# Splitting the 512-column matmuls of a two-block transformer kernel into pairs of 256, with their input laid out anew

## The reference

```python
# layer A and layer B, 512 tokens
qkv = x @ w_qkv                       # 1024 -> 3072
mix = attention(q, k, v) @ w_o        # 1024 -> 1024
x = layer_norm(DEEPNORM_ALPHA * x + mix, ...)
gate, up = jnp.split(x @ w_in, 2, axis=-1)      # 1024 -> 2 * 2816
x = layer_norm(DEEPNORM_ALPHA * x + (silu(gate) * up) @ w_out, ...)
# the second model: 16 meta tokens + 512 tokens = 528 columns
```

## Time and profile before

| | |
|---|---|
| median of 3 runs | 2583.98 us (2582.28 to 2586.15) |
| the profiled execution's own time | 2582.26 us |
| its span, first to last instruction | 2580.5 us |
| TensorE busy | 2535.2 us, 98% |
| VectorE busy | 1622.0 us, 63% |
| ScalarE busy | 1163.0 us, 45% |
| mean granted TensorE clock | 0.997 |

### The profile page before, as it was taken

The page is one execution under the profiler, slowest core; times in us unless marked ns, Lnnn a source line. Parts: engine busy times, 40 slices in busy tenths (PEclk is TensorE's granted clock), DMA queues, the critical chain, the costliest instruction groups (busy, mean ns, idle before and its releaser), DMA issues.

```text
span 2580.5 us, 44843 instructions
## 1 busy us (share of the span) xinstructions
PE 2535.2 (98%) x19310; PEld 2300.2 (89%) x19310; DVE 1622.0 (63%) x2784; ACT 1163.0 (45%) x1924; POOL 168.7 (7%) x218
## 2 busy tenths in 40 slices
PE   9999999999999999999999999999999999999998
PEld 7777889889877888989899899999999989999998
DVE  6767746457566665546766456666675754766666
ACT  4554533335455443334554444434454534544443
POOL 0000200100000110110000001001000000200100
PEclk9999999999999999999999999999999999999999
DMA  5221955974322492795311149359652112954965
GB/s 193 89 63 70 260 143 161 293 185 147 108 73 74 151 253 84 261 257 161 141 67 65 60 142 263 98 170 289 158 189 92 65 64 103 260 144 136 293 174 162
DMA packets 104280, 397.39 MB, mean 154 GB/s; under 512 B 10401, under 2 KB 12705, under 8 KB 84241
## 3 DMA queue, kind: packets, MB, share of 16 engines
q1 hardware_dynamic: 60400, 249.07, 28.1%
q0 software_dynamic: 42960, 143.88, 23.7%
q10 hardware_dynamic: 720, 1.57, 0.2%
HBM read 383.87 MB, written 133.30 MB: 200 GB/s over the span
## 4 chain that ended last, share of the span: by engine, by line
PE 89%; DVE 6%; ACT 3%; DMA 1%; issue 1%; SPq 0%; DVEq 0%; ACTq 0%
PE P L684 60%; PE P L1014 13%; PE P L802 4%; PE P L780 3%; PE P L691 2%; DVE WL L2115 2%; ACT WH L1473 1%; PE P L814 1%; DMA raw<-in_wts 1%; PE P L1111 1%; PE P L1132 1%; PE P L1224 1%; PE P L828 1%; PE P L860 1%; DVE X L2210 0%
## 5 line engine op out<-in xcount | busy, mean ns | idle before, releaser
L684 PE MATMUL P<-XH,WL 128*128 128x264 f32 (+3 forms) x3080 | 843.0, 323 | 15.3 <-DVE XL L2448 6.9
L684 PE MATMUL P<-XL,WH 128*128 128x264 f32 (+3 forms) x3080 | 823.1, 316 | 0.0
L684 PE MATMUL P<-XH,WH 128*128 128x264 f32 (+3 forms) x3080 | 820.4, 315 | 0.0
L2115 DVE TENSOR_TENSOR WL<-raw,WH 128x1024 fp32r<-128x1024 f32 (+2 forms) x533 | 573.7, 1079 | 326.5 <-ACT WH L1473 325.0
L1473 ACT ACTIVATE WH<-raw 128x1024 fp32r<-128x1024 f32 (+2 forms) x533 | 497.9, 940 | 467.7 <-PE P L684 228.7
L684 PEld LDWEIGHTS P<-XH,WL 128*128 128x128 f32 x3080 | 520.4, 188 | 65.6 <-DVE XL L2448 9.8
L684 PEld LDWEIGHTS P<-XH,WH 128*128 128x128 f32 x3080 | 518.9, 189 | 37.8
L684 PEld LDWEIGHTS P<-XL,WH 128*128 128x128 f32 x3080 | 519.0, 188 | 36.6
L1014 PE MATMUL P<-GHH,WL 128*128 128x264 f32 (+1 forms) x616 | 176.2, 286 | 9.7 <-DVE WL L2115 9.7
L1014 PE MATMUL P<-GHL,WH 128*128 128x264 f32 (+1 forms) x616 | 175.4, 285 | 0.0
L1014 PE MATMUL P<-GHH,WH 128*128 128x264 f32 (+1 forms) x616 | 175.3, 285 | 0.0
(11 more groups left out here) (372 smaller groups left out, 3803.6 us busy)
## 6 DMA issues: line engine op xcount, KB each, us to landing
raw<-in_wts SPq DMA_DIRECT2D x151, 1024.0 KB, 5.1
sums<-in_quads POOLq DMA_DIRECT2D x32, 1152.0 KB, 28.4
sums<-in_quads POOLq DMA_DIRECT2D x32, 960.0 KB, 24.1
sums<-in_quads POOLq DMA_DIRECT2D x16, 1536.0 KB, 19.1
raw<-sums SPq DMA_DIRECT2D x64, 384.0 KB, 3.4
sums<-in_quads POOLq DMA_DIRECT2D x16, 1280.0 KB, 12.9
raw<-sums SPq DMA_DIRECT2D x64, 320.0 KB, 3.1
raw<-in_wts SPq DMA_DIRECT2D x48, 384.0 KB, 3.6
```

The lines of the kernel that those rows point to most:

```text
L684: ins = nc.tensor.matmul(P[:, a:a + x1 - x0], wb[:, s, 128 * k:128 * k + 128], xb[:, kx, x0 - c0:x1 - c0], start=start and i == 0, stop=st ...
L2115: nc.vector.tensor_tensor(WL[:, u % NS, 0:length(u)], raw_of(u), WH[:, u % NS, 0:length(u)].bitcast(F), ALU.subtract).then_inc(*dve.up("wl ...
```

## The change

Three things. `one(b)` gives two segments of 256 columns in place of one of 512, in the same bank. The input gets views `XHf` and `XLf` on the memory of `XH` and `XL`, with rows of 512 columns (2048 bytes) for the eight steps; `XHf` starts where `XH` does, `XLf` 128 columns (512 bytes) into `XL`, so that the low part is 17408 bytes (17 KiB) behind the high one. All writers and readers of the input in the 512-token stages take these views; the stages on 528 tokens keep `XH` and `XL`. Only the first matmul of a bank clears it.

```diff
 def one(b):
-    return [(512 * b, META, T)]
+    return [in_bank(b, a0, a1) for a0, a1 in HV]
...
+        XHf, XLf = (x[:, :, :].rearrange("p k t -> p (k t)")[:, a:a + 4096].rearrange("p (k t) -> p k t", t=512)
+                    for x, a in ((XH, 0), (XL, 128)))
...
                 for i, (wb, xb) in enumerate(((WL, xh), (WH, xl), (WH, xh))):
                     for a, x0, x1 in segs:
+                        first_of_bank = all(a // 512 != b // 512 for b, x2, _ in segs if x2 < x0)
                         ins = nc.tensor.matmul(P[:, a:a + x1 - x0], wb[:, s, 128 * k:128 * k + 128],
-                                               xb[:, kx, x0 - c0:x1 - c0], start=start and i == 0, stop=stop and i == 2,
-                                               skip_group_check=loose)
+                                               xb[:, kx, x0 - c0:x1 - c0], start=start and i == 0 and first_of_bank, stop=stop and i == 2,
+                                               skip_group_check=loose or len({b // 512 for b, _, _ in segs}) < len(segs))
...
+                xh, xl, c0 = (XHf, XLf, META) if one_bank else (XH, XL, 0)
...
-                        part(u, k, [seg(0, 0)], XH, XL, k, 0, k == 0, k == 7, True)
+                        part(u, k, [seg(0, 0)], xh, xl, k, c0, k == 0, k == 7, True)
...
-                            for i, (xb, wb) in enumerate(((XL, WH), (XH, WL), (XH, WH))):
-                                ins = nc.tensor.matmul(o, xb[:, k, c0:c1], wb[:, (u + k // 4) % NS, 256 * (k % 4):256 * (k % 4) + 256],
+                            for i, (xb, wb) in enumerate(((XLf, WH), (XHf, WL), (XHf, WH))):
+                                ins = nc.tensor.matmul(o, xb[:, k, c0 - META:c1 - META], wb[:, (u + k // 4) % NS, 256 * (k % 4):256 * (k % 4) + 256],
...
-                        tile(U + 6 * g + n, one(b), XH, XL, slot)
+                        tile(U + 6 * g + n, one(b), XHf, XLf, slot, META)
...
-                        tile(up_unit(U, n), one(b), XH, XL)
+                        tile(up_unit(U, n), one(b), XHf, XLf, c0=META)
...
-                nc.scalar.activation(XH[:, m, a:b], tmp[m % 4][:, a:b], ACT.Identity, bias=par("ln_b", 16 * (s // 2) + 8 * (s % 2) + m)
+                nc.scalar.activation(XHf[:, m, a - META:b - META], tmp[m % 4][:, a:b], ACT.Identity, bias=par("ln_b", 16 * (s // 2) + 8 * (s % 2) + m)
```

More of the change, by code:

```diff
@@ L705, in early @@
                         pe.wait_ge(*at("xl", 0, k))
-                        ins = part(u + n, k, regions[n], XH, XL, k, 0, k == 0, k == 7)
+                        ins = part(u + n, k, regions[n], XHf, XLf, k, META, k == 0, k == 7)
                     ins.then_inc(*pe.up("unit", u + n))
             def early_halves(u, seg, ver, one_bank, between, late=()):
+                xh, xl, c0 = (XHf, XLf, META) if one_bank else (XH, XL, 0)
                 pe.wait_ge(*at("wlo", u))
@@ L715, in early_halves @@
                         pe.wait_ge(*at("xl", ver, k, 0))
-                        part(u, k, [seg(0, 0)], XH, XL, k, 0, k == 0, k == 7, True)
+                        part(u, k, [seg(0, 0)], xh, xl, k, c0, k == 0, k == 7, True)
                     if k >= 2:
                         pe.wait_ge(*at("wlo", u + 1))
-                        part(u + 1, k - 2, [seg(1, 0)], XH, XL, k - 2, 0, k == 2, k == 9, True)
+                        part(u + 1, k - 2, [seg(1, 0)], xh, xl, k - 2, c0, k == 2, k == 9, True)
                     if k < 8:
@@ L723, in early_halves @@
                 for k in range(8):
-                    part(u + 2, k, [seg(2, 0)], XH, XL, k, 0, k == 0, k == 7, True)
+                    part(u + 2, k, [seg(2, 0)], xh, xl, k, c0, k == 0, k == 7, True)
                     between(1, k)
@@ L730, in early_halves @@
                         for n in ns:
-                            ins = part(u + n, k, [seg(n, 1)], XH, XL, k, 0, k == 0 and not one_bank, k == 7, True)
+                            ins = part(u + n, k, [seg(n, 1)], xh, xl, k, c0, k == 0 and not one_bank, k == 7, True)
                             if k == 7:
@@ L2081, in act_program @@
                 act.wait_ge(x_loaded[k], 16)
-                nc.scalar.activation(XH[:, k, C1], X[:, k, C1], ACT.Copy).then_inc(*act.up("xh", 0, k))
+                nc.scalar.activation(XHf[:, k, :], X[:, k, C1], ACT.Copy).then_inc(*act.up("xh", 0, k))
                 if k == 2:
@@ L2226, in split @@
                 dve.wait_ge(*at("xh", s + 1, m, hf))
-                nc.vector.scalar_tensor_tensor(XL[:, m, a:b], tmp[m % 4][:, a:b], par("ln_b", 16 * (s // 2) + 8 * (s % 2) + m),
-                                               XH[:, m, a:b].bitcast(F), ALU.add, ALU.subtract).then_inc(*dve.up("xl", s + 1, m, hf))
+                nc.vector.scalar_tensor_tensor(XLf[:, m, a - META:b - META], tmp[m % 4][:, a:b], par("ln_b", 16 * (s // 2) + 8 * (s % 2) + m),
+                                               XHf[:, m, a - META:b - META].bitcast(F), ALU.add, ALU.subtract).then_inc(*dve.up("xl", s + 1, m, hf))
             def layer_norm(s, U):
@@ L2243, in layer_norm @@
                     else:
-                        nc.vector.scalar_tensor_tensor(X[:, m, C1], XH[:, m, C1].bitcast(F), float(ALPHA), pb, ALU.mult, ALU.add
+                        nc.vector.scalar_tensor_tensor(X[:, m, C1], XHf[:, m, :].bitcast(F), float(ALPHA), pb, ALU.mult, ALU.add
                                                        ).then_inc(*dve.up("reshi", s, m))
                         dve.wait_ge(*at("reshi", s, m))
-                        nc.vector.scalar_tensor_tensor(X[:, m, C1], XL[:, m, C1].bitcast(F), float(ALPHA), X[:, m, C1],
+                        nc.vector.scalar_tensor_tensor(X[:, m, C1], XLf[:, m, :].bitcast(F), float(ALPHA), X[:, m, C1],
                                                        ALU.mult, ALU.add).then_inc(*dve.up("res", s, m))
@@ L2468, in feed_forward @@
                         k = n // 2 - 2
-                        nc.vector.tensor_tensor(X[:, k, C1], XH[:, k, C1].bitcast(F), XL[:, k, C1].bitcast(F), ALU.add
+                        nc.vector.tensor_tensor(X[:, k, C1], XHf[:, k, :].bitcast(F), XLf[:, k, :].bitcast(F), ALU.add
                                                 ).then_inc(*dve.up("xs", l, k))
@@ L2603, in partial @@
                 dve.wait_ge(*at("apv", 2, 1))
-                nc.vector.scalar_tensor_tensor(parts[n], XH[:, n, C1].bitcast(F).rearrange(halves, c=256), float(ALPHA),
+                nc.vector.scalar_tensor_tensor(parts[n], XHf[:, n, :].bitcast(F).rearrange(halves, c=256), float(ALPHA),
                                                bank(n).rearrange(halves, c=256), ALU.mult, ALU.add).then_inc(*dve.up("part", s, n))
                 dve.wait_ge(*at("part", s, n))
-                nc.vector.scalar_tensor_tensor(parts[n], XL[:, n, C1].bitcast(F).rearrange(halves, c=256), float(ALPHA), parts[n],
+                nc.vector.scalar_tensor_tensor(parts[n], XLf[:, n, :].bitcast(F).rearrange(halves, c=256), float(ALPHA), parts[n],
                                                ALU.mult, ALU.add).then_inc(*dve.up("partlo", s, n))
@@ L2994, in dve_program @@
                 dve.wait_ge(*at("xh", 0, k))
-                nc.vector.tensor_tensor(XL[:, k, C1], X[:, k, C1], XH[:, k, C1].bitcast(F), ALU.subtract).then_inc(*dve.up("xl", 0, k))
+                nc.vector.tensor_tensor(XLf[:, k, :], X[:, k, C1], XHf[:, k, :].bitcast(F), ALU.subtract).then_inc(*dve.up("xl", 0, k))
                 if k == 2:
```

4 lines of the change are left out of this document (2 added, 2 removed).

## The result

The changed kernel takes 2607.57 us in the median (2606.93 to 2610.72), the kernel before 2584.24 (2582.28 to 2586.15), four executions each: a ratio of 1.009, with a 95% interval of 1.0078 to 1.0101. It is slower by 23.3 us; forecast were +17.5 us and 2601 us. The profiled execution took 2606.93 us, its span is 2605.1 us, 24.6 more than before, at the same mean granted clock of 0.997.

The account below looks back on a forecast made before the run. TensorE was taken as the bound, busy 2535.2 of 2580.5 us; 16.8 + 0.8 + 0.6 - 0.7 = +17.5 us gave 2601 us. Its own range was 2592 to 2609 us; for eight times in ten, from 2566 to 2609.

Parts of the forecast that it names:

- points 5, 6 and 7: More matmuls and loads to issue, the other engines' work, and waits: each priced at nothing.
- Point 1: Dense tiles on `XH`: 2664 matmuls of 512 columns become 5328 of 256 at 119 ns, +16.8 us.
- at 120: Matmuls at equal phases take 120 ns: dense tiles +22.1 us, `values_of` +1.6, `early_halves` +1.0.
- Points 2 and 3: `values_of` (768 matmuls) and `early_halves` (432), all at 119 ns: +0.8 us and +0.6 us.
- Point 4: Output projections: 288 matmuls of 512 columns become pairs, half at the fast and half at the slow speed, -0.7 us.
- The fast speed: Rival: uniform rows run at 113.3 ns throughout, -20.7 us, 2563 us; chance 0.27 for throughout or nearly.
- The mixture: Rival: speed depends on the last disturbance, stages fall on either side, about -2 us, 2582 us; chance 0.11.
- One price per matmul: Rival: each extra matmul costs a fixed 3.7 ns, +10.9 us, 2595 us; chance 0.17 together with the plain slow speed.

Follow-up runs that it names:

- pad64: The changed kernel with 64 unused bytes ahead of the weights, which move to phase 192 while the input stays at 128; 2580.23 us, ratio 0.9986 to the kernel before.
- shift64: The changed kernel with the input views started 48 columns into `XH` and 112 into `XL`, so streamed rows have phase 64; 2582.14 us, ratio 0.9982 to the kernel before.
- spacing: The changed kernel with `XLf` at the start of `XL`, so the low part is 16.5 KiB behind the high one, phases equal as before; 2607.85 us.
- layout_only: The changed kernel without the split: input rows of 512 columns at phase 128, dense tiles one segment of 512; 2575.44 us, ratio 0.9953 to the kernel before.
- layout_out_g1: The new layout unsplit, plus 64 bytes ahead of `OH` and `OH2`, and the last down-projection's input in `FH`, `FL`; 2572.86 us, ratio 0.9946 to the kernel before.
- split_only: The changed kernel without the new layout: two segments of 256 columns, input rows of 528 columns as before; 2590.85 us, ratio 1.0017 to the kernel before.
- pad_low: The changed kernel with 64 unused bytes between `WH` and `WL`, so low weights stand 64 ahead of the input and high ones equal; 2608.24 us.

## Why the prediction was right, and where its sum fell short

**The forecast time.** 2601 us were forecast and 2607.57 measured, inside the range but 1.4 us under its upper end, which was the sum with all equal phases at 120 ns and the output projections slow. The mechanism was right and the main term too small.

**The bound and the mechanism.** TensorE was the path and its distances decided; waits, other engines and the number of instructions (points 5, 6 and 7) came out at nothing, as the groups show. That equal phases are a bad distance for 256 columns was read from eight matmuls of `values_of` and is what the chip does in thousands of them; `pad64` and `shift64` show that the distance between the two addresses is the cause, and `spacing` that the KiB isn't.

**Point 1, the dense tiles: mis-sized.** I took 119 ns between 117.5 and 120; the settled value is 120.0. 8.3 ns over 2664 matmuls are 22.1 us instead of 16.8, the sum's own case "at 120", and this is most of what it lacked. Of the two rows for equal phases, both 4 distances long and behind a pause, the one without movement, 88.75 to 89.23, was the settled value. The other, at 117.5, was the start behind a pause: the changed kernel shows it too, with 117, 118, 120, 120, 117 and 118 ns from 84.87 us on and 120 after that. The prediction had the right reason in hand ("repeated without moving") and then took a value between the two.

**Points 2 and 3.** `values_of` rose from 117.8 to 119.8 ns, over the 696 distances that stand close together +1.4 us for 0.8; the halves by 2.1 ns over 432, +0.9 us for 0.6. Both lie near the sums "at 120".

**Point 4, the output projections:** -0.35 us for -0.7. The matmuls of 256 columns on `OH` and `OL`, the halves among them, averaged 116.1 ns, 232.2 for a pair against 233.3 for one of 512, so neither speed throughout, as assumed.

**The term that was missing.** The down-projections on `FH` aren't touched, and the sum gave them nothing. Their mean rose from 113.9 to 115.3 ns over 1829 distances, +2.5 us: two of the long stretches fell to 117.8. The prediction had shown that a disturbance sets this speed and that it is kept, but didn't carry it to untouched code behind the changed one. It isn't an effect of this change with a fixed sign. The same mean was 115.7 in `layout_only`, 114.8 in its repetition and 113.7 in `layout_out_g1`. It would be worth several microseconds between executions of one kernel, but it isn't the only thing that differs: of 25 executions of the kernel before, the five slowest (2589.92 to 2590.84 us) are just the five whose mean granted clock was 0.995 or less, where the others had 0.996 or 0.997.

With 21.4 (the mean over all dense pairs, 119.9 ns a matmul), 1.4, 0.9, -0.35 and 2.5 the rows give 25.9 us; the span grew by 24.6. The 1.3 us between are spread over attention and the second model and weren't followed up.

**The rivals.** The fast speed (2563 us) came in no stretch of the changed kernel's input, but it is what the same code takes 64 bytes further on, in three of the four long stretches of each run. So that rival asked the right question. The mixture (2582) is just what pad64 and shift64 are, at 2580 and 2582. One price per matmul (2595) lies 4 us above `split_only`, and as a law it fails: the price of the second matmul is 2.3 ns on drifting rows and 13.3 on rows of equal phase.

**What no part of the prediction saw** is that the layout by itself is a gain. It priced the layout through 256-column matmuls only, since the change had no others. The expectation for `layout_only` was too high for the same reason: it took the 512-column price from rows at other distances.

**What the Trainium skill's rules made of it.** The 2.5 ns per matmul of the Trainium skill, TensorE: Matmul & The Clock Gate, Part 1, would have given 2591 us. The kernel took 2607.57, and the distance beyond the columns was between 6.6 and 13.3 ns here, 106.7 being 256 columns at 2.4 GHz. The independent read ports of the Trainium skill, same page, Part 2, leave no room for a distance that hangs on two addresses; `shift64` against the changed kernel, 6.7 ns a matmul by where the streamed rows start, disagrees with it. The 107 ns that the Trainium skill gives there for a load of 128 columns are in no row: a load's record takes 188 ns in the stretch of 512 columns (90.26 us over 481), so at 113 or 120 ns from start to start such records overlap and their row is full.

## What stays open

What meets what inside the memory isn't shown. That the load of a stationary operand is one side of it is shown by `pad64`; that it is the load of just the next matmul isn't, since `pad_low` fits that only in part. What chooses between 113.3 and 117.8 ns at 64 ahead or behind isn't shown either: pauses come before both, and the same code at the same addresses took both in one execution. Longer or artificial pauses weren't tried, nor were the 264-column rows of the second model laid out anew.

## What to carry to other kernels

Where TensorE is the bound and each matmul loads its own weights, take the distance from start to start in every family of long stretches, before and after, and set it beside the two operands' addresses modulo 256 bytes: here a pad of 64 bytes was worth as much as the whole change. Measure a layout and a split apart; the layout that is best for one width (equal phases, 226.7 ns at 512 columns) was the worst for the other (120.0 at 256). And where a short stretch of before already shows the new situation, take the value that doesn't move over a mean of what is there.

## What the runs showed of the hardware

- The distance of two matmuls depends on where loaded and streamed operand stand to each other modulo 256 bytes, by up to 6% at 256 columns (113.3 to 120.0 ns) and 3% at 512 (226.7 to 233.4). Equal phases are the worst for 256 and the best for 512, and 64 ahead at its faster speed the other way round.
- At 64 bytes ahead the same code has two speeds at 256 columns, 113.3 and 117.8 ns, kept for up to 1047 matmuls. At 64 behind both occur too (113.4 ns for 95 distances and 117.7 elsewhere in `pad64`), though every long stretch there had 117.8. Equal phases and 128 had neither as a settled speed.
- Two of 256 columns are not one of 512: at equal phases they cost 13.3 ns more (240.0 against 226.7), while at 64 ahead a pair at its faster speed (226.6) costs 6.8 less than the 233.4 of one.
